# Turning the first and last chunk of six feed-forwards by DMA transposes, and a new order of their last units

## The chip, the cores and the metric

One Trainium2 chip; the kernel uses one of its cores. The metric is device time in microseconds of one launch, the median of three runs. The times in rows of the trace come from one profiled execution.

## What is computed

Two stacks of layers over 256 rows (tokens) of width 1024, in float32. The first stack has two layers (feed-forward, a mixer of three branches, feed-forward), the second two layers (another mixer, cross-attention to a memory, feed-forward). So there are six feed-forwards, and the change is in these alone:

```python
D_MODEL = 1024
SEQ = 256
D_FF = 2816
def swiglu_ffn(h, w_gate, w_up, w_down):
    return (jax.nn.silu(h @ w_gate) * (h @ w_up)) @ w_down
x = x + 0.5 * rms_norm(swiglu_ffn(rms_norm(x, g_pre), w_gate, w_up, w_down), g_post)
```

(In the second stack the factor 0.5 is absent.) The other stages are projections, attentions, a convolution, scans and norms, and none of their code is touched but for one call each on the load queue.

## The kernel before

**Precision.** Every float32 weight tile is split in a high part (`w_hi`, float32r, written by ScalarE in `high`, L1225) and a low part (`w_lo`, the difference, written by VectorE in `weight_low`, L1798). The activations are split in the same way. A product is three matmuls: high by high, high by low, low by high (`products`, L521, whose matmul is L541).

**Units.** The weights come in units of 1 MB (128 partitions by 2048 float32), numbered over the whole program. SyncE's queue loads a unit in two DMAs (L403); `raw` has 5 slots, and the load of unit u waits until unit u-5 has been multiplied. `w_hi` has 4 slots, so `high` of unit u waits until unit u-4 has been multiplied (`high(L, k + AHEAD)` with AHEAD = 3 is called three units ahead). Each unit is 24 matmuls of 512 columns on TensorE.

**A feed-forward** has 33 units: the hidden width of 2816 is cut in 11 chunks of 256 columns, and a chunk has two gate-and-up units (the two halves of the contraction over 1024) and one down unit. k0 is its first unit, `end` (k0 + 32) its last, and f its number from 0 to 5. For chunk c the work goes round the engines:

- TensorE: `gate_up` (L640), two units into the PSUM banks 6 and 7, the gate in the left half, the up product in the right. Before it starts it waits for `hid_ready` of chunk c-1, because both banks are read until then.
- ScalarE: `silu` (L1313): two activations of 128x256 from PSUM (L1316), once the second of the two units is done.
- VectorE: `hidden` (L1878): two products of 128x256 from PSUM (L1881) into `hid`, which gives `hid_ready`.
- The turn: `hid` has tokens on partitions, and the down product needs the hidden columns there. For chunks 1 to 9 VectorE separates the float32 in 16-bit halves (`part`, L1890, its copy L1893), SyncE's queue issues two DMA transposes (`turn_halves`, L434, L438), and VectorE puts the halves together again (`join`, L1896, two copies L1902). For chunks 0 and 10 TensorE does it: `hidden` on TensorE (L645) is four transposes of 128x128 (L650) into bank 4.
- ScalarE writes the high part of the turned chunk (L1326), VectorE the low part (`hidden_low`, L1888), which gives `gT_ready`.
- TensorE: `down` (L654), one unit that accumulates into banks 0 to 3.

**The order.** Nothing schedules this at run time: each engine has its own order, written out by hand, and semaphores tie them. On TensorE it is: first pair (gate and up of chunk 0, `first_pair`, L569), then gate and up of chunk 1 with `hidden(0)` between its two units, the down unit of chunk 0, and for c = 2 to 9 gate and up of c, then down of c-1. The end:

```python
            end, c = k0 + U_FFN - 1, NCHUNK - 1
            gate_up(L, end - 3, c)
            down(L, end - 1, c - 1, False, first(lambda t: hidden(c) if t else None))
            down(L, end, c, False, rows_lead(L, j + 1), hT, (0, 1), lambda t: (ffn_out, 1))
```

So a down unit stands between any two pairs of gate and up. The four transposes of chunk 10 lie in the middle of the down unit of chunk 9. In the last unit `rows_lead` (L613) slips in the first turn of the next stage's rows (`norm_turn`, L605, L609), which waits for the norm at the end of the feed-forward (`norm_out`).

In VectorE's `ffn` (L1875) the order at the start is `hidden(0)`, low part of unit k0+4, `hidden_low(0)`, low parts of k0+5 and k0+6, `hidden(1)`. In the fourth feed-forward (the second of the first stack's last layer) the cross-attention's memory is prepared in the same place: `memory_rows` on VectorE (L2189, L2194), `memory_turn` on TensorE (L921, 16 transposes at L927), `memory_high` on ScalarE, `memory_low` on VectorE (L2197, L2202); TensorE waits for the last of `memory_low` ahead of the down unit of chunk 0.

Of the kernel before, what the change touches and what calls it, by code (L numbers as in the profile page):

```python
# [29 lines left out]
ALU = mybir.AluOpType  # L30
# [3 lines left out]
P = 128  # L34
# [117 lines left out]
def _program(ctx, nc, d, out, counted):  # L152
# [171 lines left out]
    silu_ready, hid_ready, hid_turned = sem("silu_ready"), sem("hid_ready"), sem("hid_turned")  # L324
# [5 lines left out]
    class Layer:  # L330
# [16 lines left out]
        def turns(self, n, c):  # L347

            return self.ffn(n) * (NCHUNK - 2) + c
# [44 lines left out]
    def _(sp):  # L394
# [46 lines left out]
        def ffn(L, n, k0, wg, wu, wd):  # L441
            for kh in range(2):
                gate_up(L, k0 + kh, kh, wg, wu, 0)

            def chunk(c, k):
                gate_up(L, k, 0, wg, wu, c)
                if c > 2:
                    turn_halves(L, n, c - 2)
                gate_up(L, k + 1, 1, wg, wu, c)
                down(L, k + 2, wd, c - 1)  # L450

            for c in range(1, NCHUNK):
                chunk(c, k0 + 3 * c - 1)
            down(L, k0 + U_FFN - 1, wd, NCHUNK - 1)
            turn_halves(L, n, NCHUNK - 2)


        for l in range(DEPTH):
            L = enter(Layer("A", l))
            ffn(L, 0, 0, d["ffn1_w_gate"], d["ffn1_w_up"], d["ffn1_w_down"])  # L460
            k = U_FFN
            for n, c0 in enumerate(A_CHUNKS.values()):
                for kh in range(2):
                    square(L, k, d["w_in"], 512 * kh, c0)
                    k += 1
                    if (n, kh) == (0, 1):
                        narrow(L, k, d["w_in"], A_LR, RANK)
# [15 lines left out]
        for l in range(DEPTH):  # L483
            L = enter(Layer("B", l))
            k = 0
            for n, c0 in enumerate(B_CHUNKS.values()):
                for kh in range(2):
                    square(L, k, d["w_in_2"], 512 * kh, c0)
                    k += 1
                    if (n, kh) == (0, 1):  # L490
                        narrow(L, k, d["w_in_2"], B_FF, 8)
# [12 lines left out]
            ffn(L, 0, k, d["w_gate_2"], d["w_up_2"], d["w_down_2"])  # L504

# [9 lines left out]
    def _(pe):  # L515
# [119 lines left out]
        def ffn(L, n, j, k0):  # L635
# [9 lines left out]
            def hidden(c):  # L645

                pe.wait_ge(hid_ready, f * NCHUNK + (c + 1))
                for i in range(2):
                    for t in range(TT):
                        mm = nc.tensor.transpose(ps[:, 4, i * T + t * P:i * T + (t + 1) * P],  # L650
                                                 hid[:, t, i * P:(i + 1) * P], ident)
                mm.then_inc(hid_turned, 1)

# [8 lines left out]
            hidden(0)  # L662
            banks_free(L, j, 1)
            if n and L.l == DEPTH - 1:
                memory_turn(L.l)
# [4 lines left out]
            for c in range(2, NCHUNK - 1):  # L670
# [4 lines left out]
            gate_up(L, end - 3, c)  # L675
            down(L, end - 1, c - 1, False, first(lambda t: hidden(c) if t else None))
            down(L, end, c, False, rows_lead(L, j + 1), hT, (0, 1), lambda t: (ffn_out, 1))
# [546 lines left out]
    def _(act):  # L1224
# [85 lines left out]
        def ffn(L, n, j, k0):  # L1310
# [8 lines left out]
            def hidden(c, dst=bT_hi[:, KD:KD + 2, :]):  # L1319
                if 0 < c < NCHUNK - 1:  # L1320
                    act.wait_ge(hid_joined, L.turns(n, c))
                    src = joined
                else:
                    act.wait_ge(hid_turned, 2 * f + (2 if c else 1))
                    src = ps[:, 4, :].rearrange("p (i t) -> p i t", i=2)
                nc.scalar.activation(dst, src, ACT.Copy).then_inc(gT_hi_ready, 1)  # L1326
# [14 lines left out]
            hidden(0)  # L1341
            if n and L.l == DEPTH - 1:
                memory_high(L.l)
            high(L, k0 + 2 + AHEAD)
            high(L, k0 + 3 + AHEAD)
            silu(L, k0 + 3, 1)
# [442 lines left out]
    def _(dve):  # L1789
# [85 lines left out]
        def ffn(L, n, j, k0):  # L1875
# [9 lines left out]
            def hidden_low(c, hi=bT_hi[:, KD:KD + 2, :], lo=bT_lo[:, KD:KD + 2, :]):  # L1885
                dve.wait_ge(gT_hi_ready, f * NCHUNK + (c + 1))
                src = joined if 0 < c < NCHUNK - 1 else ps[:, 4, :].rearrange("p (i t) -> p i t", i=2)
                V.tensor_tensor(lo, src, flat(hi), ALU.subtract).then_inc(gT_ready, 1)  # L1888
# [7 lines left out]
            def join(c):  # L1896

                dve.wait_ge(halves_turned, 32 * L.turns(n, c))
                src = halves_T.rearrange("p t (b i) n -> p t b i n", b=2)
# [733 lines left out]
```

## Time and profile before

| | |
|---|---|
| median of three runs | 2055.99 us (2055.59 to 2056.2) |
| profiled execution, its own time | 2055.71 us |
| its span, first to last instruction | 2053.9 us |
| TensorE, matmuls busy | 2036.4 us |
| VectorE busy | 1385.7 us |
| ScalarE busy | 1120.8 us |
| bytes moved by DMA, mean rate | 382.69 MB, 186 GB/s |
| granted TensorE clock, mean | 0.999 |

Busy time is the union of an engine's instructions; matmuls overlap, so TensorE's says how long it had some matmul in flight. 1.8 us of the execution's time lie outside the span.

### The profile page before, as it was taken

Reading aid. Unit: us, or ns where it says so; the run is one execution under the profiler, and the core shown is the slowest. Engines: PE = TensorE matmul, PEld = TensorE weight load, DVE = VectorE, ACT = ScalarE, POOL = GpSimd, SP = SyncE. Lnnn points to the kernel's source line nnn. Section 1 sums busy time; section 2 is a strip of 40 time slices with the busy share of each in tenths; the row PEclk is TensorE's granted clock in tenths of the full one; section 3 lists DMA queues with packets and bytes.
Section 4 is the critical chain, followed back from the end, with each engine's and each line's share of the span. In section 5 each row is a group of like instructions: output and inputs, shape, how many; then the busy total and the mean of one; then the engine's idle time right before and its main releaser. Section 6 shows DMA issues by size and latency. Waiting matters only on the chain.

```text
span 2053.9 us, 24653 instructions
## 1 busy us (share of the span) xinstructions
PE 2036.4 (99%) x9886; PEld 1683.2 (82%) x9886; DVE 1385.7 (67%) x1801; ACT 1120.8 (55%) x1386; POOL 0.2 (0%) x4
## 2 busy tenths in 40 slices
PE   8999999999999999999999999999999999999998
PEld 6888887888888888887888888898888888988887
DVE  6666798766657666798776656866665668566564
ACT  6445657664446445666564446646644466565443
POOL 0000000000000000000000000000000000000000
PEclk9999999999999999999999999999999999999999
DMA  8765654456766675554567655443576554445763
GB/s 273 210 205 170 208 177 145 167 193 203 217 200 205 208 212 169 196 171 144 180 212 211 212 175 200 164 145 135 179 219 206 181 197 156 149 143 186 204 217 113
DMA packets 302193, 382.69 MB, mean 186 GB/s; under 512 B 74672, under 2 KB 210176, under 8 KB 302080
## 3 DMA queue, kind: packets, MB, share of 16 engines
q1 hardware_dynamic: 298112, 369.88, 56.8%
q10 hardware_dynamic: 3968, 11.24, 1.6%
q8 instruction: 78, 1.28, 0.2%
q14 instruction: 35, 0.29, 0.1%
HBM read 365.86 MB, written 1.05 MB: 179 GB/s over the span
## 4 chain that ended last, share of the span: by engine, by line
PE 97%; DMA 1%; ACT 1%; DVE 1%; issue 0%; SPq 0%; DVEq 0%; ACTq 0%
PE ps L541 86%; PE ps L1072 2%; PE ps L609 1%; PE ps L632 1%; PE ps L1175 1%; PE ps L1156 1%; DMA raw<-in_ffn_w_up 1%; DVE x L1846 1%; PE ps L805 1%; DMA raw<-in_w_in 0%; PE ps L690 0%; PE ps L1020 0%; ACT w_hi L1234 0%; PE ps L986 0%; PE ps L650 0%
## 5 line engine op out<-in xcount | busy, mean ns | idle before, releaser
L1805 DVE TENSOR_TENSOR w_lo<-raw,w_hi 128x2048 fp32r<-128x2048 f32 x342 | 773.4, 2266 | 308.9 <-ACT w_hi L1234 307.7
L1234 ACT ACTIVATE w_hi<-raw 128x2048 fp32r<-128x2048 f32 x342 | 648.0, 1897 | 448.1 <-PE ps L541 327.2
L541 PE MATMUL ps<-w_hi,hT_hi 128*128 128x512 f32 x2000 | 788.9, 394 | 1.8 <-DVE w_lo L1805 1.8
L541 PE MATMUL ps<-w_lo,hT_hi 128*128 128x512 f32 x2000 | 779.7, 390 | 0.0
L541 PE MATMUL ps<-w_hi,hT_lo 128*128 128x512 f32 x2000 | 757.7, 391 | 0.0
L541 PEld LDWEIGHTS ps<-w_hi,hT_hi 128*128 128x128 f32 x2000 | 375.9, 188 | 83.9 <-issue 6.6
L541 PEld LDWEIGHTS ps<-w_hi,hT_lo 128*128 128x128 f32 x2000 | 375.2, 188 | 78.8
L541 PEld LDWEIGHTS ps<-w_lo,hT_hi 128*128 128x128 f32 x2000 | 376.1, 188 | 74.6
L541 PE MATMUL ps<-w_hi,bT_hi 128*128 128x512 f32 x640 | 250.9, 392 | 0.0
L541 PE MATMUL ps<-w_hi,bT_lo 128*128 128x512 f32 x640 | 249.3, 389 | 0.0
L541 PE MATMUL ps<-w_lo,bT_hi 128*128 128x512 f32 x640 | 249.2, 389 | 0.0
L1316 ACT ACTIVATE scratch<-ps,stat 128x256 f32<-128x256 f32 x132 | 55.4, 471 | 188.1 <-PE ps L541 188.0
L541 PEld LDWEIGHTS ps<-w_hi,bT_hi 128*128 128x128 f32 x640 | 120.2, 188 | 25.5 <-issue 0.7
L541 PEld LDWEIGHTS ps<-w_hi,bT_lo 128*128 128x128 f32 x640 | 120.1, 188 | 25.4
L541 PEld LDWEIGHTS ps<-w_lo,bT_hi 128*128 128x128 f32 x640 | 120.2, 188 | 24.3
L1881 DVE SCALAR_TENSOR_TENSOR scratch<-ps,stat,scratch 128x256 f32<-128x256 f32 x132 | 57.8, 479 | 112.3 <-ACT scratch L1316 112.3
L1902 DVE COPY scratch<-scratch 128x512 uint16<-128x512 uint16 x108 | 43.6, 460 | 88.1 <-DMA scratch<-scratch 88.1
L2039 DVE SCALAR_TENSOR_TENSOR scratch<-scratch,pack 128x256 f32<-128x256 f32 x240 | 98.0, 479 | 0.0
L1370 ACT ACTIVATE scratch<-ps,stat 128x512 f32<-128x512 f32 (+1 forms) x84 | 51.3, 662 | 79.7 <-PE ps L541 79.6
L1266 ACT ACTIVATE hT_hi<-ps,gains_T 128x128 fp32r<-128x128 f32 x192 | 54.8, 379 | 24.3 <-PE ps L609 23.2
L1819 DVE SCALAR_TENSOR_TENSOR hT_lo<-ps,gains_T,hT_hi 128x128 fp32r<-128x128 f32 x192 | 52.7, 343 | 18.2 <-ACT hT_hi L1266 18.2
L1893 DVE COPY scratch<-scratch 128x1024 uint16<-128x1024 uint16 x54 | 37.5, 694 | 1.9
(298 smaller groups left out, 1312.6 us busy)
## 6 DMA issues: line engine op xcount, KB each, us to landing
raw<-in_w_in SPq DMA_DIRECT2D x160, 512.0 KB, 4.5
raw<-in_ffn_w_gate SPq DMA_DIRECT2D x88, 512.0 KB, 3.7
raw<-in_ffn_w_up SPq DMA_DIRECT2D x88, 512.0 KB, 4.7
raw<-in_ffn_w_down SPq DMA_DIRECT2D x88, 512.0 KB, 4.3
raw<-in_w_gate SPq DMA_DIRECT2D x44, 512.0 KB, 3.7
raw<-in_w_up SPq DMA_DIRECT2D x44, 512.0 KB, 4.7
raw<-in_w_down SPq DMA_DIRECT2D x44, 512.0 KB, 4.2
raw<-in_w_out SPq DMA_DIRECT2D x32, 512.0 KB, 4.4
```

The costliest lines, as they stand in the source:

```text
L541: mm = nc.tensor.matmul(bank(t, half), act[:, tiles[i], t * P:(t + 1) * P], w, start=start and (i, n) == steps[0], stop=stop and (i, n) == ...
L1072: mm = nc.tensor.matmul(out_, parts[part][:, i, c * P:(c + 1) * P], act[:, first + i, :], start=start and (i, n) == (0, 0) and c % 2 == 0, ...
L1234: nc.scalar.activation(w_hi[:, u % HIGH_RING, cols], raw[:, slot, cols], ACT.Copy).then_inc(high_ready, 1)
L1266: nc.scalar.activation(hT_hi[:, 4 * kh + c, t * P:(t + 1) * P], ps[:, 6 - 2 * t + kh, c * P:(c + 1) * P], ACT.Copy, scale=pre_gain(L, j, 4 ...
L1316: silu_t = nc.scalar.activation(sil[:, t, :], ps[:, bank + t, 0:FC], ACT.Silu, scale=rstd_in[:, t:t + 1])
L1370: last = nc.scalar.activation(dst[:, t, :], src[:, t, :], func, scale=scale[:, t:t + 1])
L1805: V.tensor_tensor(w_lo[:, slot, cols], raw[:, slot, cols], flat(w_hi[:, u % HIGH_RING, cols]), ALU.subtract).then_inc(low_ready, 1)
L1819: turned_low = V.scalar_tensor_tensor(hT_lo[:, c, t * P:(t + 1) * P], ps[:, 6 - 2 * t + kh, (c % 4) * P:(c % 4 + 1) * P], pre_gain(L, j, c ...
L1881: up = V.scalar_tensor_tensor(hid[:, t, :], ps[:, bank + t, FC:2 * FC], rstd_in[:, t:t + 1], sil[:, t, :], ALU.mult, ALU.mult)
L1893: V.tensor_copy(halves, pairbuf[:, 512:1024].bitcast(U16).rearrange("p (t n b) -> p t b n", t=TT, b=2)).then_inc(halves_ready, 1)
L1902: both = V.tensor_copy(dst[:, t, :, :, :], src[:, t, :, :, :])
L2039: V.scalar_tensor_tensor(conv_y[:, c, :], src, w[:, c, i:i + 1], conv_y[:, c, :], ALU.mult, ALU.add).then_inc(*done("conv_taps", f"tap{i}_ ...
```

## The change

The four TensorE transposes go for chunks 0 and 10 of each feed-forward; both chunks take the way of the others, through `part`, two DMA transposes, and `join`. On TensorE the gate and up units of chunk 10 move in front of the down unit of chunk 8. The load queue follows that order. The transposes of chunk 10 are issued on it after the first two units of the next stage. The last two chunks' turned parts go to the tiles 0 to 3 of `hT`.

```diff
         def turns(self, n, c):
-            return self.ffn(n) * (NCHUNK - 2) + c
+            return self.ffn(n) * NCHUNK + (c + 1)
...
# SyncE's load queue
             def chunk(c, k):
                 gate_up(L, k, 0, wg, wu, c)
                 if c > 2:
                     turn_halves(L, n, c - 2)
                 gate_up(L, k + 1, 1, wg, wu, c)
-                down(L, k + 2, wd, c - 1)
-
-            for c in range(1, NCHUNK):
+                if c == 2:
+                    turn_halves(L, n, 0)
+
+            for c in range(1, NCHUNK - 1):
                 chunk(c, k0 + 3 * c - 1)
-            down(L, k0 + U_FFN - 1, wd, NCHUNK - 1)
-            turn_halves(L, n, NCHUNK - 2)
+                if c < NCHUNK - 2:
+                    down(L, k0 + 3 * c + 1, wd, c - 1)
+            end, c = k0 + U_FFN - 1, NCHUNK - 1
+            for kh in range(2):
+                gate_up(L, end - 4 + kh, kh, wg, wu, c)
+            turn_halves(L, n, c - 2)
+            for i in range(3):
+                down(L, end - 2 + i, wd, c - 2 + i)
+            turn_halves(L, n, c - 1)
...
# in each mixer, after the first two units of the stage
                     if (n, kh) == (0, 1):
+                        turn_halves(L, 0, NCHUNK - 1)
                         narrow(L, k, d["w_in"], A_LR, RANK)
...
# TensorE
             first_pair(L, j, k0, 4, (early, early))
             square(L, k0 + 2, hT, 0, mid, True, False)
-            hidden(0)
             banks_free(L, j, 1)
             if n and L.l == DEPTH - 1:
+                pe.wait_ge(hid_ready, f * NCHUNK + 1)
                 memory_turn(L.l)
...
-            for c in range(2, NCHUNK - 1):
+            for c in range(2, NCHUNK - 2):
                 gate_up(L, k0 + 3 * c - 1, c)
                 down(L, k0 + 3 * c + 1, c - 1, False)
             end, c = k0 + U_FFN - 1, NCHUNK - 1
-            gate_up(L, end - 3, c)
-            down(L, end - 1, c - 1, False, first(lambda t: hidden(c) if t else None))
-            down(L, end, c, False, rows_lead(L, j + 1), hT, (0, 1), lambda t: (ffn_out, 1))
+            gate_up(L, end - 6, c - 1)
+            gate_up(L, end - 4, c)
+            down(L, end - 2, c - 2, False)
+            down(L, end - 1, c - 1, False, None, hT, (0, 1))
+            down(L, end, c, False, rows_lead(L, j + 1), hT, (2, 3), lambda t: (ffn_out, 1))
...
# ScalarE
             silu(L, k0 + 1, 0, 0)
             high(L, k0 + 1 + AHEAD)
-            hidden(0)
+            high(L, k0 + 2 + AHEAD)
             if n and L.l == DEPTH - 1:
                 memory_high(L.l)
-            high(L, k0 + 2 + AHEAD)
             high(L, k0 + 3 + AHEAD)
+            hidden(0)
             silu(L, k0 + 3, 1)
...
             high(L, end - 3 + AHEAD)
-            hidden(c - 1)
+            silu(L, end - 3, c)
+            hidden(c - 1, hT_hi[:, 0:2, :])
             high(L, end - 2 + AHEAD)
-            silu(L, end - 2, c)
             high(L, end - 1 + AHEAD)
-            hidden(c, hT_hi[:, 0:2, :])
+            hidden(c, hT_hi[:, 2:4, :])
             root(L, j)
...
# VectorE
             hidden(0, 0)
+            part(0)
             if n and L.l == DEPTH - 1:
                 memory_rows(L.l)
             weight_low(L, k0 + 1 + AHEAD)
-            hidden_low(0)
+            weight_low(L, k0 + 2 + AHEAD)
             if n and L.l == DEPTH - 1:
                 memory_low(L.l)
-            weight_low(L, k0 + 2 + AHEAD)
+            join(0)
+            hidden_low(0)
             weight_low(L, k0 + 3 + AHEAD)
             hidden(1)
             part(1)
...
-            end = k0 + U_FFN - 1
-            join(NCHUNK - 2)
+            end, c = k0 + U_FFN - 1, NCHUNK - 1
+            join(c - 1)
             weight_low(L, end - 3 + AHEAD)
-            hidden_low(NCHUNK - 2)
+            hidden(c)
+            part(c)
+            hidden_low(c - 1, hT_hi[:, 0:2, :], hT_lo[:, 0:2, :])
             weight_low(L, end - 2 + AHEAD)
-            hidden(NCHUNK - 1)
+            join(c)
+            hidden_low(c, hT_hi[:, 2:4, :], hT_lo[:, 2:4, :])
             weight_low(L, end - 1 + AHEAD)
-            hidden_low(NCHUNK - 1, hT_hi[:, 0:2, :], hT_lo[:, 0:2, :])
```

## Rows read from the trace of the kernel before

**Rows 1.** The page, part 1: busy time, share of the span and instructions.

```profile
PE 2036.4 (99%) x9886; PEld 1683.2 (82%) x9886; DVE 1385.7 (67%) x1801; ACT 1120.8 (55%) x1386; POOL 0.2 (0%) x4
```

**Rows 2.** The page, part 4: the chain that ended last, by engine.

```profile
PE 97%; DMA 1%; ACT 1%; DVE 1%; issue 0%; SPq 0%; DVEq 0%; ACTq 0%
```

**Rows 3.** Waits of PE: who waited for whom, us in total, times, longest.

```profile
PE ps L541 <- DVE w_lo L1805: 1.8, 1, 1.8
```

**Rows 4.** Groups of instructions on PE: busy us, mean ns, idle before.

```profile
L650 PE MATMUL ps<-const,scratch 128*128 128x128 f32 x48 | 7.2, 271 | 0.0
```

**Rows 5.** The chain in order of time: start us, us, what; first and fourth feed-forward.

```profile
31.55 0.44 PE ps L650 x4
31.99 155.10 PE ps L541 x684
...
187.08 0.44 PE ps L650 x4
187.52 5.60 PE ps L541 x24
...
1065.24 1.75 PE ps L927 x16
```

**Rows 6.** Timeline, first feed-forward, chunk 9: start us, us, engine, line, what.

```profile
167.65 0.39 PE L541 MATMUL ps<-w_hi,hT_lo 128*128 128x512 f32 x1
167.88 0.39 PE L541 MATMUL ps<-w_hi,bT_hi 128*128 128x512 f32 x1
...
168.08 0.84 ACT L1316 ACTIVATE scratch<-ps,stat 128x256 f32<-128x256 f32 x2 [3.46 <-PE ps L541]
...
168.95 0.88 DVE L1881 SCALAR_TENSOR_TENSOR scratch<-ps,stat,scratch 128x256 f32<-128x256 f32 x2 [2.02 <-ACT scratch L1316]
169.86 0.69 DVE L1893 COPY scratch<-scratch 128x1024 uint16<-128x1024 uint16 x1
```

**Rows 7.** Timeline of PE at the program's first matmuls, after its one wait for VectorE.

```profile
13.31 0.50 PE L541 MATMUL ps<-w_hi,hT_hi 128*128 128x512 f32 x1 [1.84 <-DVE w_lo L1805]
13.65 0.40 PE L541 MATMUL ps<-w_lo,hT_hi 128*128 128x512 f32 x1
```

**Rows 8.** Timeline, first feed-forward, from chunk 0's product to its down unit.

```profile
28.43 0.88 DVE L1881 SCALAR_TENSOR_TENSOR scratch<-ps,stat,scratch 128x256 f32<-128x256 f32 x2 [4.16 <-ACT scratch L1316]
...
30.16 2.29 DVE L1805 TENSOR_TENSOR w_lo<-raw,w_hi 128x2048 fp32r<-128x2048 f32 x1 [0.86 <-ACT w_hi L1234]
...
34.46 4.50 DVE L1805 TENSOR_TENSOR w_lo<-raw,w_hi 128x2048 fp32r<-128x2048 f32 x2 [1.11 <-ACT w_hi L1234]
...
37.32 0.39 PE L541 MATMUL ps<-w_hi,bT_hi 128*128 128x512 f32 x1
```

**Rows 9.** The lines L1326 and L1888, turned chunks: ns min/median/max, first and last start.

```profile
L1326 ACT ACTIVATE bT_hi<-scratch x54: 609/613/636, 49.3 to 2028.1; 128x512 fp32r<-128x512 f32 x54
L1888 DVE TENSOR_TENSOR bT_lo<-scratch,bT_hi x54: 683/685/690, 51.6 to 2030.4; 128x512 fp32r<-128x512 f32 x54
```

**Rows 10.** Timeline, issue of two DMA transposes and the join after them, two chunks.

```profile
170.58 2.50 SPq L438 DMA_TRANSPOSE scratch<-scratch  x2
...
175.85 0.81 DVE L1902 COPY scratch<-scratch 128x512 uint16<-128x512 uint16 x2 [2.80 <-DMA scratch<-scratch]
...
648.52 2.50 SPq L438 DMA_TRANSPOSE scratch<-scratch  x2
...
652.28 0.80 DVE L1902 COPY scratch<-scratch 128x512 uint16<-128x512 uint16 x2 [1.58 <-DMA scratch<-scratch]
```

**Rows 11.** Timeline, fourth feed-forward: the memory's rows and low parts, chunk 0's down unit.

```profile
1064.10 1.29 DVE L2194 SCALAR_TENSOR_TENSOR scratch<-scratch,stat 128x1024 f32<-128x1024 f32 x1
...
1068.10 2.48 DVE L2202 TENSOR_TENSOR bT_lo<-ps,bT_hi 128x512 fp32r<-128x512 f32 x4
...
1072.32 0.39 PE L541 MATMUL ps<-w_hi,bT_hi 128*128 128x512 f32 x1
```

**Rows 12.** Stretches: busy us (count) of PE, PEld, DVE, ACT, POOL; PEclk, DMA share, GB/s.

```profile
13.00:17.00 4.00, 3.69 (x11) 2.87 (x12) 4.00 (x14) 4.00 (x10) 0.00 (x0) 0.65 1.10 348
```

More of the change, by code:

```diff
@@ L323, in _program @@
     ffn_out, root_loaded, const_loaded = sem("ffn_out"), sem("root_loaded"), sem("const_loaded")
-    silu_ready, hid_ready, hid_turned = sem("silu_ready"), sem("hid_ready"), sem("hid_turned")
+    silu_ready, hid_ready = sem("silu_ready"), sem("hid_ready")
     halves_ready, halves_turned, hid_joined = sem("halves_ready"), sem("halves_turned"), sem("hid_joined")
@@ L439, in turn_halves, with ffn @@
                     halves_turned, 16)
-        def ffn(L, n, k0, wg, wu, wd):
+        def ffn(L, n, k0, wg, wu, wd, ffn_ahead=None):
             for kh in range(2):
                 gate_up(L, k0 + kh, kh, wg, wu, 0)
+            if ffn_ahead:
+                turn_halves(*ffn_ahead, NCHUNK - 1)
             def chunk(c, k):
@@ L449, in chunk @@
                 gate_up(L, k + 1, 1, wg, wu, c)
-                down(L, k + 2, wd, c - 1)
-            for c in range(1, NCHUNK):
+                if c == 2:
+                    turn_halves(L, n, 0)
+            for c in range(1, NCHUNK - 1):
                 chunk(c, k0 + 3 * c - 1)
-            down(L, k0 + U_FFN - 1, wd, NCHUNK - 1)
-            turn_halves(L, n, NCHUNK - 2)
+                if c < NCHUNK - 2:
[7 more added lines that the diff above has]
+            turn_halves(L, n, c - 1)
         for l in range(DEPTH):
             L = enter(Layer("A", l))
-            ffn(L, 0, 0, d["ffn1_w_gate"], d["ffn1_w_up"], d["ffn1_w_down"])
+            ffn(L, 0, 0, d["ffn1_w_gate"], d["ffn1_w_up"], d["ffn1_w_down"], (Layer("A", l - 1), 1) if l else None)
             k = U_FFN
@@ L490, in _ @@
                     if (n, kh) == (0, 1):
+                        turn_halves(*((Layer("B", l - 1), 0) if l else (Layer("A", DEPTH - 1), 1)), NCHUNK - 1)
                         narrow(L, k, d["w_in_2"], B_FF, 8)
@@ L504, in _ @@
             ffn(L, 0, k, d["w_gate_2"], d["w_up_2"], d["w_down_2"])
+        turn_halves(Layer("B", DEPTH - 1), 0, NCHUNK - 1)
         for t in range(TT):
@@ L643, in gate_up @@
                     square(M, k + kh, hT, 4 * kh, mid, kh == 0, kh == 1)
[L645 to L652, printed above, removed]
             def down(M, k, c, start, before=None, left=bT, tiles=(KD, KD + 1), mark=None):
@@ L1319, in hidden @@
             def hidden(c, dst=bT_hi[:, KD:KD + 2, :]):
[L1320 to L1326, printed above, removed]
+                act.wait_ge(hid_joined, L.turns(n, c))
+                nc.scalar.activation(dst, joined, ACT.Copy).then_inc(gT_hi_ready, 1)
             def chunk(M, k, c):
@@ L1886, in hidden_low @@
                 dve.wait_ge(gT_hi_ready, f * NCHUNK + (c + 1))
-                src = joined if 0 < c < NCHUNK - 1 else ps[:, 4, :].rearrange("p (i t) -> p i t", i=2)
-                V.tensor_tensor(lo, src, flat(hi), ALU.subtract).then_inc(gT_ready, 1)
+                V.tensor_tensor(lo, joined, flat(hi), ALU.subtract).then_inc(gT_ready, 1)
             def part(c):
@@ L1898, in join @@
                 dve.wait_ge(halves_turned, 32 * L.turns(n, c))
+                if c == NCHUNK - 1:
+                    dve.wait_ge(gT_ready, f * NCHUNK + c)
                 src = halves_T.rearrange("p t (b i) n -> p t b i n", b=2)
```

## The prediction

> **What bounds the kernel now.** I read the busy times first: TensorE has a matmul in flight for 2036.4 us, 99% of the span, while VectorE has 67% and ScalarE 55% [rows 1]. Then the chain that ended last: 97% of it is TensorE [rows 2]. Then TensorE's own waits: after the start it has one that matters, 1.8 us at its first matmuls [rows 3]. In none of the six feed-forwards does it wait for a hidden chunk, its turn or its split. So the kernel is as long as TensorE's list of work, plus any wait on it; what VectorE, ScalarE and the load queue do costs nothing until TensorE has to wait for it. The steady pace is in the chain: 684 matmuls in 155.10 us [rows 5], 0.227 us each, 5.44 us for a unit of 24. The sum below is TensorE's gain against its new waits.
>
> **What is removed.** 48 transposes, four in each of 12 places. Each shows 271 ns [rows 4], but they overlap. The chain charges 0.44 us for four, at both places of a feed-forward [rows 5]. The place at the end costs more than that: the 24 matmuls behind it take 5.60 us where 24 steady ones take 5.44, 0.16 us more [rows 5]. A feed-forward therefore gives back 0.44 + 0.44 + 0.16 = 1.04 us, six give 6.2 us. The Trainium skill ("TensorE: Matmul & The Clock Gate", Part 4: PE-mode transpose) gives about 275 ns for a 128x128 transpose within a kernel. The duration in the trace agrees; but if each of the 48 were worth that, the gain would be 13.2 us, and the chain's 0.11 us a piece speaks against it. The sum goes by the chain.
>
> **What is moved: gate and up of chunk 10, in front of the down unit of chunk 8.** Gate and up of every chunk write the same banks 6 and 7, and TensorE waits for `hid_ready` of the chunk before. Until now a down unit of 5.44 us lay between, and covered silu and product. The diff leaves banks and wait as they are and takes that cover away between chunks 9 and 10. Rows 6 let one read what shows then. The last matmul of gate and up of chunk 9 starts at 167.65 and the next, of the down unit, at 167.88. Silu starts at 168.08, when the unit is done, and takes 0.84. The product starts at 168.95 and ends 0.88 later, at 169.83. Both engines were idle before (3.46 and 2.02 us) and have nothing else in the way, so nothing earlier can be had. TensorE, released some 0.04 us later, starts its next matmul at 169.87 instead of 167.88: 1.99 us. A stream that starts anew also loses a little: after the one wait in the trace the second matmul follows at 0.34 us and not at 0.227 [rows 7], 0.11 more, and I add 0.06 for somewhat slow ones behind it. That makes 2.16 us for each feed-forward and **13.0 us for six**. The bounds: 1.9 (no loss at the restart) and 2.4 us (a restart that loses twice as much and more). The down units of 8 and 9, now back to back, take the place of one that went; their number is the same, and nothing comes back for the wait.
>
> **What is added at the end: chunk 10 by DMA.** Count from the end of its gate and up. Silu and product take 1.75 us, `part` 0.69 [rows 6], the transposes 3.8 to 5.3 from issue to join (652.28 - 648.52 and 175.85 - 170.58), `join` 0.8 [rows 10]: 7.0 to 8.5 us. The high part stands behind `high(end+2)`, which waits for the first down unit at 5.44 and is shorter than the 2.29 of a unit's low part [rows 8]: it ends before 7.8. High part 0.61 and low part 0.69 [rows 9] follow the later of the two: ready at 9.1 to 9.9 us. TensorE has two down units to do, 10.9 us, and does not wait. This cover is what the new order buys. I put it at nothing; without it, as in the old order with 5.4 us of cover, it would cost 9.1 - 5.4 = 3.7 us or more each. Chunk 9's turn has a whole gate-and-up pair more than before. On the load queue the transposes (2.5 us to issue two [rows 10]) come after the next stage's second unit; behind them stands a load that has to wait for the first down unit, at 5.44, and by then they are issued (2.4 + 2.5 = 4.9). Nothing.
>
> **What is added at the start: chunk 0 by DMA.** In the first feed-forward the product ends at 29.31 [rows 8]. `part` ends at 30.03, before VectorE's next split could start (30.16), so it is free. The queue issues the transposes at 30.06, the gate and up load in front having gone out at the end of the first pair. The load behind them waits for the unit that ends at 31.55 anyway [rows 5] and goes about 1 us later; it has a turn of five units to spare. Two low parts of weights from 30.16 take 4.50, to 34.6 [rows 8]; the transposes need 3.76, to 33.8. So VectorE, not the DMA, sets the join: 34.6 + 0.8 = 35.4, then 0.61 and 0.69 with 0.03 us between each [rows 9]: ready at 36.8. TensorE wants its first down matmul at 37.32 [rows 8] less the 0.44 that it gained: 36.88, and its weight load 0.23 before that, 36.65. That is late by 0.2 us: **0.2 for each of five, 1.0 us**. Bounds: 0, and 1.0 us where the transposes need 5.27 [rows 10] (35.3 instead of 34.6 at the join, and a restart); 12 of the 54 turns of before took over 4.5 us, the space there is. `hidden(1)` then ends about 0.3 us later than before, with 5 us to spare.
>
> **The fourth feed-forward** has the memory's work on VectorE in the same place. There `part` (0.69) stands in front of `memory_rows`, whose last row ends at 1065.39 [rows 11] and would end at 1066.1. TensorE's second eight transposes for the memory wait for it; they need half of 1.75 [rows 5] and end at 1067.0, where all 16 ended before: the 0.44 gained are lost. Then VectorE goes on: two low parts 4.5 (1070.5), `memory_low` 2.48 (1072.9) [rows 11], join 0.8, high 0.61, low 0.69 and the hops: 1075.1. TensorE would start the down unit at 1072.32 [rows 11]: 2.8 us, and 0.1 for the restart. Together **3.4 us**. Bounds: 2.5 and 4.2 (late transposes are hidden here; one split more or less in front is not).
>
> **Sum.** 2055.71 - 6.2 + 13.0 + 1.0 + 3.4 = 2066.9 us for an execution like the profiled one (span 2053.9 and 1.8 outside). The median of the three runs lies 0.3 us above that execution, so 2067.
>
> **Rivals.** (a) *Late transposes.* The DMA, not VectorE, sets chunk 0's join: the transposes are in flight with the loads issued at the end of the first pair. Each of five feed-forwards then loses 1.0 instead of 0.2: +4.0, 2071 us. For it: 12 of 54. Against: table load, silu, product and `part` lie between these loads and the transposes, and more than three quarters of the turns of before took less than 4.5.
>
> (b) *The wait is paid in part.* If silu and product of chunk 9 cost TensorE only some 1.0 us, for instance because instructions already loaded run on, the sum is 6 x 1.16 = 7.0 lower: 2060, at the edge of no change. Against: the wait stands in TensorE's own list and the count is reached only with the second product.
>
> (c) *The clock falls.* TensorE stands still seven times for 2 to 3 us. In this trace the clock was low only at the start, 0.65 of full in 13 to 17 us [rows 12], that is for a part at 1.2 instead of 2.4 GHz; 0.35 of 4 us is 1.4 us of full speed lost. If each stop brought the same, 7 x 1.4 = 9.8 us: 2077. Against: no stop in the middle of the trace shows it, though none there is as long. The Trainium skill ("TensorE: Matmul & The Clock Gate", HAM oscillation) warns that long idle gaps between matmuls bring the low clock back; no run so far shows where that begins here.
>
> (d) *Faster.* The mechanism is that product 9 is ready when TensorE comes to chunk 10, and only the removal is left. The place is the `hid_ready` wait in the last `gate_up`; the point from which it decides is a wait of (6.2 - 4.4) / 6 = 0.3 us a feed-forward. With none the time is 2055.7 - 6.2 + 4.4 = 2053.9. For it: no `gate_up` waits today. Against: each has 5.44 us of cover, and rows 6 show that 2 us are needed.
>
> **How the numbers follow.** The sum as worked out has 0.75, (a) 0.12, (b) 0.05, (c) 0.05, (d) 0.03. The forecast is the sum's, 2067. With the bounds of the wait (-1.6, +1.4), the start (-1.0, +4.0) and the fourth (-0.9, +0.8) the range is 2063.5 to 2072, which takes in (a); outside stay (b), (c), (d) and some of the tails. A measurement can tell about 0.2% (4 us) from no change. So: slower 0.91, same 0.06 ((b) and a little), faster 0.03.
>
> **What would show each step.** No rows of L650 are left, and the 684 steady matmuls are broken. Among TensorE's waits a new one for the product L1881 stands, six times 2.0 us: that is the main step; without it I am wrong. A wait for L1888 of 2.8 us in the fourth feed-forward, and up to 0.2 in the five others, at chunk 0 alone. L1902 and L1893 have 132 and 66 instructions. The down units of 8, 9 and 10 follow one another with no wait for L1888; one there would mean that chunk 10's turn is longer than I count. The granted clock behind each stop stays at full; if not, (c).

## The result, and the profile after

| | before | changed |
|---|---|---|
| median, us | 2055.79 (4 runs, 2054.48 to 2056.2) | 2070.99 (4 runs, 2070.79 to 2071.8) |
| profiled execution, us | 2055.71 | 2070.89 |
| its span, us | 2053.9 | 2069.1 |
| TensorE matmuls busy, us | 2036.4 | 2036.6 |

The ratio is 1.0075, 95% interval 1.0062 to 1.0087: 15.2 us or 0.75% slower. Forecast were 2067 us (11.2 more than the profiled execution of before) and a range of 2063.5 to 2072.

The page of the changed kernel, part 1, and the first line of its chain, answer to [rows 1, 2]:

```profile
PE 2036.6 (98%) x9838; PEld 1680.0 (81%) x9838; DVE 1402.5 (68%) x1837; ACT 1121.5 (54%) x1386; POOL 0.2 (0%) x4
...
PE 95%; DVE 2%; ACT 2%; DMA 1%; issue 1%; SPq 0%; ACTq 0%; DVEq 0%
```

TensorE has 48 instructions less and the same busy time. Busy time is no measure of its work here: the transposes overlapped their neighbours, and matmuls at a lower clock, of which more below, count as busy. What grew is the time in which the chain runs over other engines. TensorE's waits say where. Before there was, besides the start, one line of more than 0.5 us [rows 3]; in the changed kernel (who waited for whom, us in total, times, longest):

```profile
PE ps L554 <- DVE scratch L1882: 11.0, 6, 1.8
...
PE ps L554 <- DVE bT_lo L1888: 2.4, 1, 2.4
PE ps L554 <- DVE w_lo L1806: 1.8, 1, 1.8
PE ps L645 <- ACT scratch L1365: 0.8, 1, 0.8
```

(L554 is the matmul that was L541, L1882 the product that was L1881.) Six waits for the product, one in each feed-forward, and one wait for a low part of a hidden chunk. The timeline of TensorE, ScalarE and VectorE around the first of the six, at the same place as [rows 6]:

```profile
169.09 0.39 PE L554 MATMUL ps<-w_hi,hT_lo 128*128 128x512 f32 x1
171.32 0.50 PE L554 MATMUL ps<-w_hi,hT_hi 128*128 128x512 f32 x1 [1.84 <-DVE scratch L1882]
171.66 0.39 PE L554 MATMUL ps<-w_lo,hT_hi 128*128 128x512 f32 x1
...
169.52 0.84 ACT L1322 ACTIVATE scratch<-ps,stat 128x256 f32<-128x256 f32 x2 [3.46 <-PE ps L554]
...
170.39 0.87 DVE L1882 SCALAR_TENSOR_TENSOR scratch<-ps,stat,scratch 128x256 f32<-128x256 f32 x2 [2.01 <-ACT scratch L1322]
```

Steady, the next matmul would have started at 169.09 + 0.227 = 169.32. It starts at 171.32, 2.00 us later; the unit's last part, silu (to 170.36) and product (to 171.26) fill that time, and the second matmul follows after 0.34 us.

The fourth feed-forward has the other wait, and something behind it. TensorE's timeline at the down unit of chunk 0, then its clock in two stretches (busy us and count of PE, PEld, DVE, ACT, POOL, then PEclk, DMA share, GB/s):

```profile
1080.76 0.47 PE L554 MATMUL ps<-w_hi,bT_hi 128*128 128x512 f32 x1 [2.41 <-DVE bT_lo L1888]
1081.06 0.40 PE L554 MATMUL ps<-w_lo,bT_hi 128*128 128x512 f32 x1
1081.30 0.52 PE L554 MATMUL ps<-w_hi,bT_lo 128*128 128x512 f32 x1
1081.62 0.63 PE L554 MATMUL ps<-w_hi,bT_hi 128*128 128x512 f32 x1
1082.04 0.63 PE L554 MATMUL ps<-w_lo,bT_hi 128*128 128x512 f32 x1
...
1084.18 0.63 PE L554 MATMUL ps<-w_hi,bT_hi 128*128 128x512 f32 x1
1084.60 0.50 PE L554 MATMUL ps<-w_lo,bT_hi 128*128 128x512 f32 x1
```

```profile
1081.00:1083.00 2.00, 2.00 (x7) 1.51 (x7) 2.00 (x2) 1.42 (x1) 0.00 (x0) 0.60 1.03 362
1083.00:1085.00 2.00, 2.00 (x7) 1.57 (x6) 1.97 (x4) 0.00 (x0) 0.00 (x0) 0.54 0.06 17
```

Seven matmuls of 0.63 us, 0.43 apart instead of 0.227, and a granted clock of 0.60 and 0.54 in the two stretches: TensorE runs at its lower level, 1.2 instead of 2.4 GHz, from 1081.6 to 1084.6, after it stood for 2.4 us. That costs seven times 0.2 and 0.2 at the two edges, about 1.6 us.

**Where the 15.2 us of the two spans lie.** The first turn of the next stage's rows is a landmark behind each feed-forward. Its rows around the second, a plain one, in the kernel before and in the changed one:

```profile
437.47 0.66 PE L609 MATMUL ps<-const,x 128*128 128x128 f32 x4
...
620.35 0.66 PE L609 MATMUL ps<-const,x 128*128 128x128 f32 x4
```

```profile
440.47 0.66 PE L622 MATMUL ps<-const,x 128*128 128x128 f32 x4
...
624.61 0.66 PE L622 MATMUL ps<-const,x 128*128 128x128 f32 x4
```

From landmark to landmark it takes 182.88 and 184.14 us, 1.26 more. The same done for all stages:

| stage | later by, us |
|---|---|
| first matmul of the program (first weights came later) | 0.6 |
| first feed-forward (1.1 of it in the first 7 us: 12 slow matmuls, before there were 7) | 2.4 |
| the four other plain feed-forwards | 1.26, 1.23, 1.26, about 1.3 |
| fourth feed-forward (with the memory) | 6.1 |
| second cross-attention (a load that came late) | 1.05 |
| the mixers and the first cross-attention | -0.1 together |

### The profile page after: what moved, and what is told of

It is laid out like the page before. It is cut to its first block, busy times and chain, and to the rows that moved or that the text cites. A ratio compares the mean times of both kernels' runs of the same rounds, so it can differ in the third digit from the quotient of the medians.

```text
span 2069.1 us, 24623 instructions
## 1 busy us (share of the span) xinstructions
PE 2036.6 (98%) x9838; PEld 1680.0 (81%) x9838; DVE 1402.5 (68%) x1837; ACT 1121.5 (54%) x1386; POOL 0.2 (0%) x4
## 3 DMA queue, kind: packets, MB, share of 16 engines
HBM read 365.86 MB, written 1.05 MB: 177 GB/s over the span
## 4 chain that ended last, share of the span: by engine, by line
PE 95%; DVE 2%; ACT 2%; DMA 1%; issue 1%; SPq 0%; ACTq 0%; DVEq 0%
PE ps L554 84%; PE ps L1078 2%; PE ps L622 1%; PE ps L645 1%; PE ps L1181 1%; PE ps L1162 1%; DMA raw<-in_ffn_w_up 1%; DVE x L1847 1%; PE ps L696 1%; PE ps L811 0%; ACT w_hi L1240 0%; DMA raw<-in_w_co 0%; DVE w_lo L1806 0%; PE ps L1026 0%; DVE scratch L1882 0%
## 5 line engine op out<-in xcount | busy, mean ns | idle before, releaser
L554 PE MATMUL ps<-w_hi,hT_hi 128*128 128x512 f32 x2048 | 808.1, 395 | 12.8 <-DVE scratch L1882 11.0
L554 PE MATMUL ps<-w_lo,hT_hi 128*128 128x512 f32 x2048 | 798.9, 390 | 0.0
L554 PE MATMUL ps<-w_hi,hT_lo 128*128 128x512 f32 x2048 | 776.3, 390 | 0.0
L554 PEld LDWEIGHTS ps<-w_hi,hT_hi 128*128 128x128 f32 x2048 | 385.3, 188 | 98.7 <-DVE scratch L1882 13.6
L554 PEld LDWEIGHTS ps<-w_hi,hT_lo 128*128 128x128 f32 x2048 | 384.1, 188 | 80.3
L554 PEld LDWEIGHTS ps<-w_lo,hT_hi 128*128 128x128 f32 x2048 | 385.4, 188 | 76.9
L554 PE MATMUL ps<-w_hi,bT_hi 128*128 128x512 f32 x592 | 232.8, 393 | 2.4 <-DVE bT_lo L1888 2.4
L554 PE MATMUL ps<-w_hi,bT_lo 128*128 128x512 f32 x592 | 231.1, 390 | 0.0
L554 PE MATMUL ps<-w_lo,bT_hi 128*128 128x512 f32 x592 | 231.1, 390 | 0.0
L554 PEld LDWEIGHTS ps<-w_hi,bT_hi 128*128 128x128 f32 x592 | 111.4, 188 | 28.1 <-issue 5.1
L1882 DVE SCALAR_TENSOR_TENSOR scratch<-ps,stat,scratch 128x256 f32<-128x256 f32 x132 | 57.8, 479 | 107.5 <-ACT scratch L1322 107.5
L554 PEld LDWEIGHTS ps<-w_hi,bT_lo 128*128 128x128 f32 x592 | 111.5, 188 | 23.5
L554 PEld LDWEIGHTS ps<-w_lo,bT_hi 128*128 128x128 f32 x592 | 111.6, 188 | 22.7
L1904 DVE COPY scratch<-scratch 128x512 uint16<-128x512 uint16 x132 | 53.1, 458 | 103.8 <-DMA scratch<-scratch 103.7
```

Of the source, the lines that this page charges most:

```text
L554: mm = nc.tensor.matmul(bank(t, half), act[:, tiles[i], t * P:(t + 1) * P], w, start=start and (i, n) == steps[0], stop=stop and (i, n) == ...
L1882: up = V.scalar_tensor_tensor(hid[:, t, :], ps[:, bank + t, FC:2 * FC], rstd_in[:, t:t + 1], sil[:, t, :], ALU.mult, ALU.mult)
L1904: both = V.tensor_copy(dst[:, t, :, :, :], src[:, t, :, :, :])
```

## The experiments

State of the theory when they began: TensorE's list is the bound, the six waits and the memory's feed-forward add up, and about 4 us more come from the lower clock, the program's start and a late load. The main rival: that the 24 extra transposes and their collisions with the loads carry most of it.

**1. Other banks for chunk 10.** The two gate-and-up units of chunk 10 write the free banks 4 and 5, and TensorE needs no wait there. ScalarE waits for chunk 9's product instead, ahead of the silu of chunk 10.

```diff
+            late = lambda t, half: ps[:, 4 + t, :]
             def gate_up(M, k, c):
-                pe.wait_ge(hid_ready, f * NCHUNK + c)
+                if c < NCHUNK - 1:
+                    pe.wait_ge(hid_ready, f * NCHUNK + c)
                 for kh in range(2):
-                    square(M, k + kh, hT, 4 * kh, mid, kh == 0, kh == 1)
+                    square(M, k + kh, hT, 4 * kh, mid if c < NCHUNK - 1 else late, kh == 0, kh == 1)
...
+            act.wait_ge(hid_ready, f * NCHUNK + c)
-            silu(L, end - 3, c)
+            silu(L, end - 3, c, 4)
...
-            hidden(c)
+            hidden(c, 4)
```

> The changed kernel, but the gate and up units of chunk 10 write the free PSUM banks 4 and 5 instead of 6 and 7, and TensorE no longer waits for the product of chunk 9 there. Theory (the six waits add up in full): 2071.0 - 6 x 2.16 = 2058 us, no wait of PE for the product L1881-L1883 left; everything else as in the changed kernel. Rival (the extra transposes and their collisions with the loads carry most of the 15 us): at most 3 us shorter, 2068 or more. Second rival (the six waits are real, but the time comes back at the next place where TensorE waits): in between, 2062 to 2066.

Measured: 2054.69 us (11 runs, 2052.71 to 2057.77), beside 2054.67 for the kernel before; ratio 1.0002 (0.9994 to 1.0011). TensorE's waits in it:

```profile
PE ps L1214 <- DMA scratch<-in_gains: 8.1, 1, 8.1
PE ps L554 <- DVE bT_lo L1892: 2.4, 1, 2.4
PE ps L554 <- DVE w_lo L1810: 1.6, 1, 1.6
PE ps L645 <- ACT scratch L1369: 0.7, 1, 0.7
```

The six are gone, and the time of the kernel before is back, with all 132 DMA transposes still in it. That refutes the rival, and the second one too (nothing comes back elsewhere). The second feed-forward takes 181.99 us from landmark to landmark, 2.15 less than in the changed kernel: 6 x 2.15 = 12.9. The medians differ by 15.3 to 16.3 (the changed kernel was timed twice), so 2.4 to 3.4 us more than the waits themselves went with them, and the theory's 2058 was that much too high. In the two profiled executions (16.5 us apart) the start explains most of it: the changed kernel has 12 slow matmuls there and this one none, which is 2.8 us. The fall of the clock in the fourth feed-forward is in both.

**2. Chunk 0 alone.** The kernel before, with `part`, transposes and `join` for chunk 0 and VectorE's and ScalarE's orders of the changed kernel at the start; the end as before.

```diff
# TensorE, the kernel before
             square(L, k0 + 2, hT, 0, mid, True, False)
-            hidden(0)
...
# load queue
                 gate_up(L, k + 1, 1, wg, wu, c)
+                if c == 2:
+                    turn_halves(L, n, 0)
                 down(L, k + 2, wd, c - 1)
```

> The kernel before with the turn of chunk 0 alone moved to DMA transposes; chunk 10 is turned by TensorE and the old order of units stands. Theory: -5 x 0.44 + 5 x 0.2 + 3.4 (fourth feed-forward) + 1.6 (the lower clock behind its long wait) = +3.8, 2059.6 us. Rival (the lower clock in the changed kernel's fourth feed-forward was chance, or belongs to the other part): +2.2, 2058.0 us, and a granted clock of 1.00 behind the wait.

Measured: 2056.90 us (11 runs) beside 2054.67; ratio 1.0009 (1.0001 to 1.0018), so +2.2, with an interval of 0.2 to 3.7 us. The wait of 2.4 us in the fourth feed-forward is there, the low clock behind it is not:

```profile
PE ps L543 <- DVE bT_lo L1890: 2.4, 1, 2.4
...
1074.00:1076.00 2.00, 1.50 (x7) 1.29 (x8) 2.00 (x2) 2.00 (x2) 0.00 (x0) 1.00 1.06 372
1076.00:1078.00 2.00, 2.00 (x11) 1.65 (x10) 1.97 (x5) 0.16 (x1) 0.00 (x0) 1.00 0.23 79
```

The rival's difference came out, but the interval all but takes in the theory's +3.8; the rows decide: the fall of the clock behind this wait is not there every time. The fourth feed-forward is 2.93 us longer in this trace; the prediction's step gave 3.4 - 0.44 = 2.96.

**3. Chunk 10 alone.** The changed kernel with chunk 0 turned by TensorE again, and ScalarE's and VectorE's orders at the start as before.

```diff
# TensorE, the changed kernel
             square(L, k0 + 2, hT, 0, mid, True, False)
+            pe.wait_ge(hid_ready, f * NCHUNK + 1)
+            for i in range(2):
+                for t in range(TT):
+                    mm = nc.tensor.transpose(ps[:, 4, i * T + t * P:i * T + (t + 1) * P],
+                                             hid[:, t, i * P:(i + 1) * P], ident)
+            mm.then_inc(hid_turned, 1)
...
# load queue
-                if c == 2:
-                    turn_halves(L, n, 0)
```

> The changed kernel with chunk 0 turned by TensorE again: the new order of the last units and the turn of chunk 10 by DMA alone. Theory: 2055.8 - 6 x 0.60 + 6 x 2.16 = 2065.2 us, six waits of PE for the product with 1.8 us of idle each, no wait for L1888 and a clock of 1.00 in all feed-forwards. Rival (the two parts hinder one another, and the sum of both parts alone does not give the whole): e2 and e3 together differ from the changed kernel's +15.2 us by over 2 us.

Measured: 2067.99 us (5 runs, 2065.07 to 2069.62) beside 2054.67; ratio 1.0063 (1.005 to 1.0077), +13.3. With the +2.2 of chunk 0 that is 15.5, the changed kernel's own difference. The profiled execution took 2065.07, what the theory gave, with six waits and the clock full behind each; the median lies 3 us higher, and the times spread over 4.5 us. The same kernel once more, for that spread:

> The same kernel as e3_chunk10_only, for its spread: its profiled execution took 2065.07 us with the clock at full behind all six waits, and its median was 2068.0. Theory (the granted clock falls behind some of these 1.84 us stops in some executions, 1.6 to 2 us each): single times between 2065 and 2070, and if the profiled execution is one of the longer ones, a group of matmuls at 0.43 us behind one or more of the six waits. Rival (the waits never bring the low clock and the spread comes from the program's start and from late loads): a longer execution whose slow groups lie at the start alone.

Measured: 2064.72 us (4 runs, 2062.94 to 2066.47) beside 2055.02; ratio 1.0054 (1.0038 to 1.0069). The profiled execution was the shortest, 2062.94, again with full clock behind all six waits, and at the program's start as well. So it did not show what a longer one contains; that came from the changed kernel's repetition below.

This second +9.7 gives 11.9 with chunk 0's +2.2, 3 us less than the changed kernel beside it (+15.0). By the medians alone, then, it is not shown that the parts add; the rival asked for a difference of over 2 us, and this one has it. The stages of the traces show it, from landmark to landmark: a plain feed-forward is 0.31 us shorter with chunk 0 alone and 1.57 longer with chunk 10 alone (foreseen were 0.24 and 1.56), together 1.26, which is what the changed kernel has; the fourth is 2.93 and 1.57 longer, together 4.5, and the changed kernel's is 4.5 in the execution without the fall of the clock there (experiment 5). Only the late load of the second cross-attention, 1 us, is in neither part and comes with both.

**4. A longer wait.** Two more products on VectorE, to unused scratch, in front of chunk 9's.

```diff
                 dve.wait_ge(silu_ready, f * NCHUNK + (c + 1))
+                if c == NCHUNK - 2:
+                    for t in range(TT):
+                        V.scalar_tensor_tensor(wide[:, 256 * t:256 * t + 256], ps[:, bank + t, FC:2 * FC],
+                                               rstd_in[:, t:t + 1], sil[:, t, :], ALU.mult, ALU.mult)
```

> The changed kernel with two further products of 128x256 on VectorE (written to unused scratch) in front of the product of chunk 9, so that each of TensorE's six waits is longer by 0.88 us, 2.7 instead of 1.84 us of idle. Theory (the waits add one to one): 2071.0 + 6 x 0.88 = 2076.3 us. Rival (from about the length of the 2.4 us wait in the fourth feed-forward on, the granted clock falls behind a wait): 1.6 us more for each where it falls, up to 2085.9 us, with matmuls at 0.43 us behind the wait and a granted clock near 0.6 in these rows.

Measured: 2079.1 us (4 runs, 2077.39 to 2079.53), ratio 1.0117 (1.0103 to 1.013); 8 to 9 us over the changed kernel. Each wait is 0.79 us longer and not 0.88 (their total is 15.8 us and was 11.0), and the third feed-forward, which has no fall of the clock, is 0.97 us longer than in the changed kernel. Six times that is 5.8, so 2 to 3 us are not the waits. In the trace the slow matmuls follow four of the six waits of 2.6 us, and the 2.4 us wait of the fourth feed-forward. One wait with them and one without:

```profile
169.45 0.80 PE L554 MATMUL ps<-w_hi,hT_hi 128*128 128x512 f32 x1 [2.63 <-DVE scratch L1886]
170.04 0.63 PE L554 MATMUL ps<-w_lo,hT_hi 128*128 128x512 f32 x1
170.47 0.63 PE L554 MATMUL ps<-w_hi,hT_lo 128*128 128x512 f32 x1
...
784.68 0.50 PE L554 MATMUL ps<-w_hi,hT_hi 128*128 128x512 f32 x1 [2.62 <-DVE scratch L1886]
785.02 0.39 PE L554 MATMUL ps<-w_lo,hT_hi 128*128 128x512 f32 x1
785.25 0.40 PE L554 MATMUL ps<-w_hi,hT_lo 128*128 128x512 f32 x1
```

The two waits are equal to 0.01 us; one brings the lower clock and the other does not. Both theories had a part of it: the longer waits are paid in full, and some of them bring a further 1.5 us, but none brings it every time. (The second feed-forward, with a fall, is 1.4 us longer than the third. Four such falls would make nearly 6; this execution had no slow matmuls at its start, where the changed kernel lost 2.8.) The Trainium skill ("TensorE: Matmul & The Clock Gate", HAM oscillation) says that long idle gaps bring the clock back to 1.2 GHz; here 2.6 us of idle do so in part of the cases.

**5. The changed kernel again.**

> The changed kernel once more, on the same chip and beside the same runs of the kernel before as the next three. Theory (15 us from two sources, the six waits and the fourth feed-forward, as the two halves alone gave +13.3 and +2.2): 15.5 us over the kernel before, 2070 to 2071 us. Rival (part of the first +15.2 was the chip of that day, such as a late weight load of the second cross-attention): 12 to 13 us over it.

Measured: 2070.02 us (4 runs, 2067.38 to 2072.6) beside 2055.02; ratio 1.0077 (1.0063 to 1.009). The difference repeats. Its profiled execution, 2071.11, has what the first lacked: slow matmuls behind two of the six waits of 1.84 us (at 171.4 and 2035.0 us), and none behind the 2.4 us wait. The first of them, and the clock of its stretches:

```profile
170.10 0.50 PE L554 MATMUL ps<-w_hi,hT_hi 128*128 128x512 f32 x1 [1.84 <-DVE scratch L1882]
170.44 0.40 PE L554 MATMUL ps<-w_lo,hT_hi 128*128 128x512 f32 x1
...
171.40 0.63 PE L554 MATMUL ps<-w_hi,hT_lo 128*128 128x512 f32 x1
171.82 0.63 PE L554 MATMUL ps<-w_hi,hT_hi 128*128 128x512 f32 x1
```

```profile
170.00:172.00 2.00, 1.90 (x7) 1.55 (x8) 1.77 (x3) 0.94 (x1) 0.00 (x0) 0.83 1.00 395
172.00:174.00 2.00, 2.00 (x7) 1.52 (x6) 1.26 (x1) 0.00 (x0) 0.00 (x0) 0.50 0.88 214
174.00:176.00 2.00, 2.00 (x9) 1.62 (x8) 0.80 (x2) 0.00 (x0) 0.00 (x0) 0.82 0.04 9
```

**6. A later low part.** On VectorE the low part of unit k0+5 goes behind `hidden_low(0)`; on ScalarE chunk 0's high part goes in front of that of unit k0+6.

```diff
             weight_low(L, k0 + 1 + AHEAD)
-            weight_low(L, k0 + 2 + AHEAD)
             if n and L.l == DEPTH - 1:
                 memory_low(L.l)
             join(0)
             hidden_low(0)
+            weight_low(L, k0 + 2 + AHEAD)
             weight_low(L, k0 + 3 + AHEAD)
```

> The changed kernel with the low part of unit k0+5 behind the low part of chunk 0 on VectorE, instead of in front of its join (and the high part of chunk 0 in front of that of unit k0+6 on ScalarE). Theory: the chain of chunk 0 in the fourth feed-forward is shorter by one low part, 2.2 us; TensorE's 2.4 us stop there shrinks to 0.2 and the clock no longer falls behind it: -2.2 - 1.6 = 3.8 us less than the changed kernel, about 2067. In the five others the join now waits for the transposes, and nothing is won or lost over 0.2 us each. Rival (the transposes are late, not VectorE): the stop stays above 1.5 us and the time within 1 us of the changed kernel's.

Measured: 2067.37 us (5 runs, 2067.27 to 2071.36) beside 2055.02; ratio 1.0069 (1.0057 to 1.0082). TensorE's stop at the down unit of chunk 0 in the fourth feed-forward is 0.24 us instead of 2.4. So VectorE's chain, not the DMA, was late there, as worked out. The median is 2.7 us less than that of the changed kernel beside it, with 3.8 foreseen; single times of the two overlap (2067.38 to 2072.6 there), so the shorter stop is shown and its worth in the median hardly. In the profiled execution the low clock came behind two of the six remaining waits. One thing was not foreseen: in the first feed-forward chunk 1's down unit now waits 1.2 us. (Experiment 8 leaves the low part in its old place there and has no such wait.)

```profile
PE ps L554 <- DVE bT_lo L1888: 1.4, 2, 1.2
```

**7. Both repairs.** Experiments 1 and 6 in one kernel, run in two sessions.

> Chunk 10 in banks 4 and 5 (as e1_other_banks) and the later low part of unit k0+5 (as e6_low_later) together. Theory: e1's 2054.7 less 3.8 = 2051 us, 3.8 us below the kernel before, which is what the removed transposes gave back (6 x 1.04 = 6.2) less the two eighths of memory transposes and small waits of chunk 0. Rival (TensorE's list is not the bound once the waits are gone; late loads are): no gain over e1, 2054 to 2055.

Measured: 2051.71 us (11 runs, 2051.27 to 2052.84) beside 2055.02; ratio 0.9986 (0.9977 to 0.9994). It is the first version that beats the kernel before (3.3 us, interval 1.2 to 4.7), and TensorE's waits are nearly gone:

```profile
PE ps L554 <- DVE w_lo L1810: 2.0, 1, 2.0
PE ps L554 <- DVE bT_lo L1892: 1.1, 2, 0.8
PE ps L645 <- ACT scratch L1369: 0.8, 1, 0.8
```

> The same kernel as e7_both, to see whether it beats the kernel before once more, and how its time spreads. Theory: 3 to 4 us below the kernel before, a ratio of 0.998 to 0.9985, and single times within 2 us, since no stop is long enough to bring the low clock. Rival (the gain was chance): within 1 us of the kernel before.

Measured: 2051.36 us (11 runs, 2050.99 to 2053.37) beside 2055.77; ratio 0.9982 (0.9973 to 0.9991). The gain holds. The spread is small, and the one long execution of the two profiled (2053.37) has seven slow matmuls at the program's start, the other (2051.56) none there.

**8. The later low part in the fourth feed-forward only**, and there `part(0)` behind the memory's rows. The cut is against the kernel of experiment 7; on ScalarE the high part of chunk 0 goes back behind that of unit k0+6 in the five others.

```diff
             hidden(0, 0)
-            part(0)
-            if n and L.l == DEPTH - 1:
-                memory_rows(L.l)
+            mem = n and L.l == DEPTH - 1
+            if mem:
+                memory_rows(L.l)
+            part(0)
             weight_low(L, k0 + 1 + AHEAD)
-            if n and L.l == DEPTH - 1:
-                memory_low(L.l)
+            if mem:
+                memory_low(L.l)
+            else:
+                weight_low(L, k0 + 2 + AHEAD)
             join(0)
             hidden_low(0)
-            weight_low(L, k0 + 2 + AHEAD)
+            if mem:
+                weight_low(L, k0 + 2 + AHEAD)
```

> As e7_both (chunk 10 in banks 4 and 5), but the low part of unit k0+5 goes behind chunk 0's only in the fourth feed-forward, and there the separation of the halves stands behind the memory's rows. Theory: the wait of 0.8 us that e7_both shows in the first feed-forward, where the tables of the rotary positions follow on VectorE, goes; in the fourth the memory's transposes no longer wait, but the chain on VectorE is as long as before, so the 0.2 us stop at the down unit of chunk 0 grows by what was gained: 0.8 us less than e7_both in all, about 2051. Rival (VectorE's chain in the fourth feed-forward is not what ends last): 1.5 us less.

Measured: 2050.97 us (11 runs, 2050.16 to 2052.95) beside 2055.77; ratio 0.9981 (0.9972 to 0.999): 0.4 us below its neighbour of experiment 7, which cannot be told from nothing. The waits moved as worked out: the one of chunk 1 in the first feed-forward is gone, but chunk 0 there has one of 0.5 us instead, and the stop in the fourth is 0.80 instead of 0.23:

```profile
1069.21 0.47 PE L554 MATMUL ps<-w_hi,bT_hi 128*128 128x512 f32 x1 [0.80 <-DVE bT_lo L1894]
```

## Why the prediction was right

**The bound** was read rightly: where TensorE does not wait, 24 more DMA transposes and 16.8 us more of VectorE's time cost nothing (experiment 1).

**The removed transposes.** In experiment 1 the second feed-forward is 0.89 us shorter than before; foreseen were 1.04 less 0.2 of new wait at chunk 0, 0.84. So the 271 ns that one transpose shows were rightly not taken as its price.

**The wait in front of chunk 10.** 2.00 us from matmul to matmul, 2.15 in all by experiment 1; foreseen 1.99 and 2.16, from rows of a kernel in which the wait did not exist. Six make 12.9 of the 15.2 us.

**Chunk 10's turn** waits for nothing. In the first feed-forward its low part ends at 191.19, 8.7 us after the unit before (182.5); foreseen were 9.1 to 9.9 with 10.9 of cover:

```profile
185.04 2.50 SPq L438 DMA_TRANSPOSE scratch<-scratch  x2
...
188.78 0.80 DVE L1904 COPY scratch<-scratch 128x512 uint16<-128x512 uint16 x2 [0.75 <-DMA scratch<-scratch]
190.50 0.69 DVE L1888 TENSOR_TENSOR hT_lo<-scratch,hT_hi 128x512 fp32r<-128x512 f32 x1 [0.92 <-ACT hT_hi L1327]
```

**Chunk 0's turn.** At its down unit TensorE has no wait in its list in the five plain ones; in the third feed-forward the first two matmuls there start 0.30 and 0.31 us after the one before (at 649.2) and not 0.227, 0.16 us late where 0.2 was foreseen. The second feed-forward's 1.26 us is 0.06 less than the step sums give (2.16 + 0.2 - 1.04 = 1.32). Rival (a), late transposes, did not occur: the join starts 4.51 to 4.56 us after the issue in all five, with VectorE busy up to it; in the last of them the transposes landed at 4.54, just in time. (Of the 54 turns of before 13, and not 12, waited for transposes of over 4.5 us.)

**The fourth feed-forward.** 2.93 us in experiment 2, 2.96 by the steps; the down unit of chunk 0 starts 2.8 us after its old place in the changed kernel as well (1080.76 against 1072.32 + 5.60 of earlier delay).

**What was missing, 4 us**, kept the result 4 us above the forecast and inside the range. The range held it by luck: its top came from the 4.0 us of rival (a), which did not occur, and with the bounds of the wait and of the fourth feed-forward alone it would have ended near 2069. (All upper bounds added give 2073.2, not 2072.) That 2071 is also rival (a)'s number means nothing.

The step that was too small is the price of a stop: it was taken as the idle time plus 0.17 us, and rival (c), the lower clock, as something that comes behind all seven stops or none, with a chance of 0.05. Both were wrong. In the profiled execution it came behind one of seven and cost 1.6 us.

Of the rest, 1.7 us are the program's start (later first weights and slow matmuls, before any changed instruction). It varies between executions of one kernel: 12 and 8 slow matmuls in the changed kernel's two profiles, 7 and none in experiment 3's, none and 7 in experiment 7's.

1.05 us are a late load in the second cross-attention. It is in the traces of all kernels in which both chunks go by DMA and in none of the others: the second half of the third `w_co` unit lands 7.5 to 7.7 us after its issue and not 6.3 to 6.5, and TensorE waits 0.7 to 0.8 us further on. No experiment was made on it, but the traces point to a cause. In these eight profiles, and in none of the four others, a packet of 16 KB of the queue q8, which the page calls "instruction", starts 4.6 to 4.7 us after that issue, while the load is in flight. The load in the changed kernel's chain (start us, us), and the packet's queue in the window 1826 to 1835 (packets, MB, share of 16 engines):

```profile
1826.65 7.69 DMA raw<-in_w_co
...
q8 instruction: 1, 0.02, 0.7%
```

The same comparison for every weight load (its time in one trace against its median in the traces where no such packet meets it): 159 loads that a 16 KB packet met at least 1 us after their issue and 1 us before their landing took 0.99 us longer in the median, 6582 that no packet met 0.00. So a change of the code can move these packets to other loads; that this one moved because of the 24 transposes was not tested.

That the excess of the medians is the clock behind the waits is shown only in single profiles (two more falls in the changed kernel's second one), not counted over the timed runs.

**The other rivals.** (b), a wait paid in part, is refuted by experiment 1: it is paid in full and more. (d) put the kernel without the wait at 2053.9; experiment 1 took the wait away by other banks and measured 2054.7. Experiments 7 and 8 went on from there: with the wait removed by other banks and the memory's chain shortened, the time is 3.3 to 4.8 us below the kernel before.

## What to carry to other kernels

Before a unit is moved, ask which waits it has been covering: the down unit between two gate-and-up pairs looked like plain work, and was the 2 us in which the banks were read. A dependence on a buffer that is about to be reused can be costed from the old trace, by adding up the readers' durations, although the wait is not in it. And where the removed work has left a buffer free (here banks 4 and 5), use it in the same change; that took back the 15 us that were lost, and with the later low part of experiment 6 it won 3 to 5 us.

## What was not expected of the hardware

- The lower TensorE clock comes behind short stops, and not every time: in the two profiles of the changed kernel the same stop of 1.84 us, the one of rows 6, brought it once and once not. Of the 30 waits with 1.84 us of idle in five profiles (the changed kernel twice, experiment 3 twice, experiment 6), 4 were followed by matmuls at 0.43 us; of the five of 2.4 us 3; of the six of 2.6 us 4; of 13 stops of 0.5 to 1.2 us none. Behind the start no slow matmul stands anywhere else in the twelve profiles. Each fall lasts 5 to 8 matmuls of 0.63 us and costs 1.4 to 1.6 us.
- The profile's clock column can miss it. At the start of the changed kernel matmuls of 0.63 us lie 0.43 us apart from 14.5 to 19.6 us, 5 and 6 of them in 2 us each, as they do where the column shows the low clock, while here it says 1.00:

```profile
14.00:16.00 2.00, 2.00 (x5) 1.61 (x6) 2.00 (x9) 2.00 (x4) 0.00 (x0) 1.00 1.10 348
16.00:18.00 2.00, 2.00 (x6) 1.52 (x6) 2.00 (x5) 2.00 (x6) 0.00 (x0) 1.00 1.14 365
```

  The same stretch of experiment 1 has 10 and 11. In the kernel before the column does show such a start (0.65 in 13 to 17 us [rows 12]). So look at the distance of the matmuls too, not at the column alone.
- This start explains part of the spread between executions of one kernel: none, 7, 8 or 12 slow matmuls were seen in the profiles, and the 12 cost 2.8 us.
